# Hybrid decoder trunk on one core: the samples' value projection of the HGRN2 layer with high and low parts stacked in one stationary tile, and its halves joined on ACT and DVE

## What is computed

```python
def hgrn2_mixer(x, s0, lb, w_in, norm_g, w_out):
    q, f, v, gate = jnp.split(x @ w_in, 4, axis=-1)        # each 2048 wide, 16 heads of 128
    forget = lb + (1.0 - lb) * jax.nn.sigmoid(f)
    log_f = jnp.log(forget)
    k = (1.0 - lb) * jax.nn.sigmoid(-f)
    q = jax.nn.silu(q)
    o, s_new = gla_chunked(q, k, v, log_f, s0)              # chunks of 16 tokens, state (16, 128, 128)
    o = o * lax.rsqrt(jnp.mean(o * o, axis=-1, keepdims=True) + EPS)
    o = o.reshape(...) * norm_g * jax.nn.silu(gate)
    return o @ w_out, s_new
```

## Time and profile before

| what | value |
|---|---|
| time, median of 3 runs (lowest to highest) | 2019.58 (2018.29 to 2019.62) |
| span of the profiled execution, first to last instruction | 2015.7 |
| mean granted TensorE clock, as a share of full speed | 0.986 |
| PE busy / DVE busy / ACT busy / POOL busy | 97% / 62% / 46% / 50% of the span |
| HGRN2 stage, from the first projection to the last output product | about 1030 to 1468 of the span |

### The profile page before, as it was taken

The page is one execution under the profiler, slowest core; times in us unless marked ns, Lnnn a source line. Parts: engine busy times, 40 slices in busy tenths (PEclk is TensorE's granted clock), DMA queues, the critical chain, the costliest instruction groups (busy, mean ns, idle before and its releaser), DMA issues.

```text
span 2015.7 us, 35615 instructions
## 1 busy us (share of the span) xinstructions
PE 1951.5 (97%) x13890; PEld 1763.9 (88%) x13890; DVE 1244.4 (62%) x2220; ACT 930.6 (46%) x1557; POOL 1008.8 (50%) x1249
## 2 busy tenths in 40 slices
PE   7999999999999999999999999999999999999997
PEld 5998989798888988897889999999998889989976
DVE  5988342426887787755147777777454157874552
ACT  3676522334555555342354444443243347674333
POOL 4776704026555655250356666566631337776602
PEclk8999999999999999999999999999999999999998
DMA  4444476535444544487353444444586344445870
GB/s 130 149 147 135 135 250 231 208 105 174 124 116 132 151 132 140 138 297 241 113 170 108 130 130 130 137 136 146 165 313 211 132 148 141 135 148 166 292 231 27
DMA packets 332615, 324.64 MB, mean 161 GB/s; under 512 B 19768, under 2 KB 313056, under 8 KB 332448
## 3 DMA queue, kind: packets, MB, share of 16 engines
q1 hardware_dynamic: 330944, 321.49, 49.8%
q10 hardware_dynamic: 1504, 0.87, 0.2%
HBM read 292.16 MB, written 29.61 MB: 160 GB/s over the span
## 4 chain that ended last, share of the span: by engine, by line
PE 75%; DVE 14%; ACT 5%; issue 2%; DMA 2%; POOL 1%; SPq 1%; DVEq 0%; ACTq 0%
PE ps L773 10%; PE ps L774 10%; PE ps L778 10%; PE ps L1458 5%; PE ps L1467 4%; PE ps L1261 3%; PE ps L1524 2%; PE ps L888 2%; PE ps L763 2%; PE ps L765 2%; PE ps L764 2%; ACT wh L1713 2%; DVE work L2543 2%; PE ps L1602 1%; PE ps L1541 1%
## 5 line engine op out<-in xcount | busy, mean ns | idle before, releaser
L1693 POOL TENSOR_TENSOR wl<-raw,wh 128x256 fp32r<-128x256 f32 x1216 | 1003.3, 860 | 979.1 <-ACT wh L1713 978.9
L1713 ACT ACTIVATE wh<-raw 128x1024 fp32r<-128x1024 f32 x304 | 311.8, 1053 | 202.1 <-PE ps L778 49.8
L773 PE MATMUL ps<-Hh,wh 128*128 128x320 f32 x1200 | 372.2, 324 | 2.8 <-DVE work L2563 0.9
L774 PE MATMUL ps<-Hl,wh 128*128 128x320 f32 x1200 | 360.4, 314 | 0.0
L773 PEld LDWEIGHTS ps<-Hh,wh 128*128 128x128 f32 x1200 | 230.0, 192 | 11.3 <-DVE work L2427 2.3
L774 PEld LDWEIGHTS ps<-Hl,wh 128*128 128x128 f32 x1200 | 230.4, 192 | 2.1
L2258 DVE TENSOR_SCALAR work<-ps 128x512 f32<-128x512 f32 (+8 forms) x220 | 100.3, 474 | 170.9 <-PE ps L871 39.8
L778 PE MATMUL ps<-Hh,wl 128*128 128x320 f32 x1200 | 201.1, 310 | 0.0
L778 PEld LDWEIGHTS ps<-Hh,wl 128*128 128x128 f32 x1200 | 183.2, 189 | 0.1
L773 PE MATMUL ps<-Oh,wh 128*128 128x320 f32 x512 | 152.2, 310 | 3.7 <-DVE Ol L3004 3.7
L774 PE MATMUL ps<-Ol,wh 128*128 128x320 f32 x512 | 151.1, 308 | 0.0
(11 more groups left out here) (439 smaller groups left out, 3922.0 us busy)
## 6 DMA issues: line engine op xcount, KB each, us to landing
raw<-rg_w_in SPq DMA_DIRECT2D x128, 256.0 KB, 3.5
raw<-hg_w_in SPq DMA_DIRECT2D x128, 256.0 KB, 4.8
raw<-ssd_w_in SPq DMA_DIRECT2D x96, 256.0 KB, 3.9
work<-cache_mem_k SPq DMA_DIRECT2D x40, 512.0 KB, 6.3
work<-cache_mem_v SPq DMA_DIRECT2D x40, 512.0 KB, 5.1
raw<-rg_w_out SPq DMA_DIRECT2D x64, 256.0 KB, 3.6
raw<-x_w_k SPq DMA_DIRECT2D x64, 256.0 KB, 3.6
raw<-x_w_v SPq DMA_DIRECT2D x64, 256.0 KB, 3.7
```

The source lines that it names most:

```text
L773: pe.matmul(ps[:, bank, 0:n], high(half, k), mh[:, k, 0:n], start=(k == 0), stop=False)
L774: pe.matmul(ps[:, bank, 0:n], high(half, k), ml[:, k, 0:n], start=False, stop=False)
L1693: ins = pool.tensor_tensor(out, src, wh[:, parted(n) % HALVES, r:r + 2].bitcast(F32), ALU.subtract)
L1713: act.activation(wh[:, nx.n % HALVES], raw[:, slot, :, half * P:(half + 1) * P], ACT.Copy).then_inc(hi_ready, 1)
```

## The change

Before group 0 ACT and DVE build `hg_stack`, [128, 8, 128]: for each k the samples' 64 high columns beside their 64 low columns. `take_v(i, 2)` then uses it as the one stationary tile, with two products for each k (by the high and by the low weights). High rows come out on partitions 0 to 63 and low rows on 64 to 127 of the same bank, and their sum is v. ACT copies partitions 64 to 127 to `hg_v[0:64]`, and DVE adds partitions 0 to 63 of PSUM (`joined`). It is now this DVE instruction that raises `hg_v_read`. The rounding into `hg_vh` moves into ACT's next round (`round_v`), and the DMA between partitions is gone. To make room, `hg_K` is laid out without its unused quarter, as 14 rows of 64 columns, and its memsets are gone.

```diff
+            hg_stack = layout.enter_context(nc.sbuf_tensor("hg_stack", [P, KD, P], F32R))
...
-        hg_K = [c(9, P), c(9, P), c(9, P), c(9, P)]
+        hg_K = [c(14, 64), c(14, 64), c(14, 64), c(14, 64)]
+        hg_K_all, hg_K_late = [K[:, 0:9, :] for K in hg_K], [K[:, 9:14, :][:, ::-1] for K in hg_K]
...
# PE, take_v
+                    if T == 2 and i == 0:
+                        pe.wait_ge(*past("hg_stacked", 2))
                     for k in range(KD):
+                        if T == 2:
+                            pe.matmul(out, hg_stack[:, k, :], both(k), start=(k == 0), stop=False)
+                            mm = pe.matmul(out, hg_stack[:, k, :], rest_of(k), start=False, stop=(k == KD - 1))
+                            continue
...
# PE, turn_and_score
-                        pe.transpose(ps[:, 5, T * P:(T + 1) * P], hg_K[2 * h + T][:, 8, :], ident[:])
+                        pe.transpose(ps[:, 5, T * P:(T + 1) * P], hg_K[2 * h + T][:, 8:10, :].rearrange("p a c -> p (a c)"), ident[:])
...
-                                               hg_K[2 * h + T][:, c, 0:w], start=True, stop=True)
+                                               hg_K[2 * h + T][:, c:18 - c:17 - 2 * c, :] if w == P else hg_K[2 * h + T][:, c, :], start=True, stop=True)
...
# ACT
+                def round_v(i):
+                    act.wait_ge(*past("hg_v_read", i + 1))
+                    act.activation(hg_vh[0:64], hg_v[0:64, 2, :], ACT.Copy).then_inc(S("hg_v_high"), 1)
...
                     if i:
+                        round_v(i - 1)
                         scores_by_query(i - 1, 0)
...
-                    act.activation(hg_v[64:P, 2, :], ps[64:P, a + 1, 0:256], ACT.Copy).then_inc(S("hg_v_read"), 1)
-                    act.wait_ge(*past("hg_v_read", i + 1))
-                    steps.did(act.activation(hg_vh[64:P], hg_v[64:P, 2, :], ACT.Copy))
-                    steps.sync()
-                    act.dma_start(hg_v[0:64, 2, :], hg_v[64:P, 2, :]).then_inc(S("hg_v_twice"), 16)
+                    act.activation(hg_v[0:64, 2, :], ps[64:P, a + 1, 0:256], ACT.Copy).then_inc(S("hg_v_low"), 1)
...
+                act.wait_ge(*past("h_high", 5 * KD))
+                act.activation(hg_stack[:, :, 0:64], Hh[:, :, SEQ:NT].bitcast(F32), ACT.Copy).then_inc(S("hg_stacked"), 1)
                 for i in range(GROUPS):
                     body(i)
+                round_v(7)
...
# DVE
                 wait("h_ready", 5 * KD)
+                copy(hg_stack[:, :, 64:P], Hl[:, :, SEQ:NT].bitcast(F32)).then_inc(S("hg_stacked"), 1)
...
-                        wait("hg_v_twice", 16 * (i + 1))
-                        did(tt(hg_v[sm, 2, :], hg_v[sm, 2, :], hg_vh[sm].bitcast(F32), SUB))
+                        wait("hg_v_high", i + 1)
+                        did(tt(hg_v[sm, 2, :], hg_v[0:64, 2, :], hg_vh[0:64].bitcast(F32), SUB))
...
+                def joined(i):
+                    wait("hg_v_low", i + 1)
+                    tt(hg_v[0:64, 2, :], hg_v[0:64, 2, :], ps[0:64, 2 * (i % 2) + 1, 0:256], ADD).then_inc(S("hg_v_read"), 1)
+
                 for i in range(GROUPS + 1):
                     a = 2 * (i % 2)
+                    if i:
+                        joined(i - 1)
                     if i < GROUPS:
                         wait("hg_g_sig", i + 1)
...
-                    if i == 0:
-                        for K in hg_K:
-                            did(dve.memset(K[:, 0:4, 64:P], 0.0))
```

More of the change, by code:

```diff
@@ L153, in trunk @@
                            ("sn_full", "xs_full"), ("sn_read", "xs_read"), ("ssq_full", "xt_full"), ("v_read", "xt_read"),
-                           ("vm_ready", "xw_ready")):
+                           ("vm_ready", "xw_ready"), ("v_high", "y_done"), ("v_low", "z_sig"), ("stacked", "z_read"),
+                           ("raw_full", "raw_full"), ("raw_read", "raw_read")):
             shared["hg_" + hgrn] = ("sd_" + ssd_, 1, GROUPS)
@@ L368, in trunk @@
         hg_v = c(3, 256)
-        c(NB + 4, P)
+        c(NB + 4 + KD, P)
         hg_kt, hg_kx = c(2, P), par[:, 3, :]
         hg_D = c(4, 72)
-        hg_K = [c(9, P), c(9, P), c(9, P), c(9, P)]
+        hg_K = [c(14, 64), c(14, 64), c(14, 64), c(14, 64)]
+        hg_K_all, hg_K_late = [K[:, 0:9, :] for K in hg_K], [K[:, 9:14, :][:, ::-1] for K in hg_K]
         hg_att = [c(NT), c(NT)]
@@ L2835, in keys @@
                         k = hg_k[:, h, T * P:(T + 1) * P].rearrange("p (c s) -> p c s", s=16)
-                        K = hg_K[2 * h + T].rearrange("p a (c s) -> p a c s", s=16)
+                        early, late = (v[2 * h + T].rearrange("p a (c s) -> p a c s", s=16) for v in (hg_K_all, hg_K_late))
                         d = hg_D[:, 2 * h + T, :].rearrange("p (a b) -> p a b", b=8)
-                        did(tt(K[:, :, 0:4], k[:, 0:4].unsqueeze(1).broadcast_to([P, 9, 4, 16]), wide(d[:, :, 0:4], 16), MUL))
-                        return tt(K[:, 4:9, 4:8], k[:, 4:8].unsqueeze(1).broadcast_to([P, 5, 4, 16]), wide(d[:, 4:9, 4:8], 16), MUL)
+                        did(tt(early, k[:, 0:4].unsqueeze(1).broadcast_to([P, 9, 4, 16]), wide(d[:, :, 0:4], 16), MUL))
+                        return tt(late, k[:, 4:8].unsqueeze(1).broadcast_to([P, 5, 4, 16]), wide(d[:, 4:9, 4:8], 16), MUL)
                     did(keys(0, 0))
```

## The result

The changed kernel takes 2052.64 (median of 4, 2050.59 to 2053.04), the kernel before 2019.60 in the same session: ratio 1.0165, 95% interval 1.0142 to 1.0188. It is slower, by 33. The profiled execution took 2053.04 with a span of 2051.3, 35.6 longer than before.

The account below looks back on a forecast made before the run. PE's own work and DVE's loop (47.5 a round) were taken as nearly equal bounds, with the late join binding afterwards. 5.2 + 1.7 + 23.8 - 1.6 + 2.7 + 1.7 = 33.5 more gave 2053; range 2034 to 2062.

Parts of the forecast that it names:

- The place of the join: Top of DVE's next round: the add releases v at 1118.3, so PE idles 5.4 and starts q 4.5 later.
- The round: Groups 1 to 7: 48.9 at full clock plus 1.7 and 0.85 for slow clock, 51.45 against 47.48.
- the 0.85: PE from take_q to v: half of 1.7 for a second slow stretch, part of which coincides with the first loss.
- The sum: Whole kernel: 5.2 + 1.7 in round 1, 23.8 in six rounds, -1.6 + 2.7 + 1.7 at the end, 33.5 more.
- The saving of the products: PE's pass for v: eight products fewer a group, 0.96 each group, 7.7 in all if nothing else held.
- rival 1: Join ready in time, loop through stores and weights binds at 47.0: faster, 2015, or 2012 if all 7.7 arrive; chance 0.06.
- the 21.0: From the end of DVE's chain through stores, loads and splits until the next v may start: 21.0.
- The clock: PE behind each stall: idle time brings a slow clock, charged at 1.7 each, so a stall costs more than its length.
- rival 2: The stall at the join comes without a slow clock behind it: 14.8 more, 2034; chance 0.17.
- Keys and memsets at nothing: DVE's eight key products stay at 7.1 a round under the new layout, and the four removed memsets were hidden.
- The 11 of slack behind ACT's half: ACT's copy to other partitions: 0.38, at most doubled, with 11 between its end and DVE's arrival, so it costs nothing.
- stack and rounding at nothing: Stack copies run during group 0's gate and q; round_v (0.4) stands where ACT waits for PE's scores: both cost nothing.

Follow-up runs that it names:

- the early join: Changed kernel with the DVE add moved into keys_of, between its first four key products and the product of q with the decays: ratio 0.994 to the kernel before.
- two products only: Kernel before without the product of low samples by high weights for the samples' v, 64 products fewer: ratio 0.9943.
- the kernel with v first: Kernel before with the block of v weights issued on SP ahead of the store and load of the second head's states: ratio 0.9956.
- the two stretches of 304.8 and 304.4: Both with the v weights' block first on SP: changed kernel with add in keys_of, 0.991; kernel before without low samples by high weights, 0.9898.
- the filled kernel: Changed kernel with 36 unused products of 192 columns on PE ahead of its wait for hg_v_read in rounds 1 to 7: ratio 1.016 to the kernel before.
- the join one step earlier: Changed kernel with the DVE add placed ahead of new_state(j, 1, 1): ratio 1.0111 to the kernel before.

## Why the prediction was right, step by step

**The place of the join: right, and shown.** The wait alone makes 1.38% of the 1.65% in the old kernel, and moving the same instruction to an earlier place turns 1.65% more into 0.6% less.

**The round: right in kind, two terms off.** The forecast was 4.4 + 21.6 + 0.4 + 22.5 at full clock, and 1.7 + 0.85 for the clock, 51.45; the measured round is 51.20. Its terms from the rows above: v to `scored` 1207.24 - 1202.85 = 4.4; DVE's chain 1229.34 - 1207.24 = 22.1 (0.5 more than taken); the join and its signal 0.46; PE from q to v 24.25, where I had 25.05. The term that was wrong is the 0.85. The second slow stretch did come in every round, but in the half where PE waits for DVE anyway. For that reason PE idled 3.8 and not 5.4, and 2.6 and not 3.6 ahead of the third `take_out`. The chain, 0.5 longer than taken, made up for more than half of the 0.85.

**The sum.** Round 1: 6.9 forecast, 8.3 measured. `take_q(1, 0)` was 6.2 later, less the 0.7 by which the whole stage began later, and 5.2 was forecast for it. The missing 1.0 is DVE's: two products of round 0, q by the decays and the one behind it, took 1.37 and 0.81 where they had taken 0.82 and 0.28, here before and then after:

```profile
1066.65 0.82 DVE L2844 TENSOR_TENSOR work<-work 128x640 f32<-128x640 f32 x1
1067.38 0.28 DVE L2845 TENSOR_TENSOR later<-work,hg_en 128x128 f32<-128x128 f32 x1
```

```profile
1067.38 1.37 DVE L2858 TENSOR_TENSOR work<-work 128x640 f32<-128x640 f32 x1
1068.67 0.81 DVE L2859 TENSOR_TENSOR later<-work,hg_en 128x128 f32<-128x128 f32 x1
```

The other 8.3 - 6.2 = 2.1 came behind `take_q`, after 7.03 of idle time, with the clock at 0.50 for 5.0 (the two rows from 1075.50); I had taken 1.7. Six rounds: 23.8 and 22.3. End: 1.1 and 1.6, and 1.7 and 1.4 behind it. Not forecast: 0.7 ahead of the stage and 1.2 after it. That the total came within 0.5 (33.5 for 33.0 on the medians) is in part luck: these terms cancel.

**The saving of the products and rival 1: mis-sized.** The forecast itself does not use this loop, as the join binds first. I held that the loop through store, load and weights binds at 47.5, so that only 5 of the 7.7 would arrive. The runs showed 10.2 on the stretch and 11.5 in time. The step that failed is the 21.0 from DVE's chain to v. I read it off round 1 alone, where `out_hs_p` landed after 5.15. With the early join it lands after 3.24, and in two of the four rounds whose v waits for its weights the way is 19.0, so that the loop is 4.4 + 22.2 + 19.0 = 45.6 (in the other two it is 19.6 and 19.8, with a slower load of weights). With two products only, the rounds that waited so are 45.7 to 46.0 long. In the kernel before, the store took 5.1 to 5.2 in three of six rounds, the one of the earlier trace rows and these two, and 3.2 to 3.7 in the others:

```profile
1260.64 5.17 DMA out_hs_p<-work
...
1356.31 5.11 DMA out_hs_p<-work
```

Those three rounds are just the ones whose v waited for the weights (47.5, 47.6 and 47.0 long). In the other three PE had no idle time, and they were 46.6, 48.1 and 48.1 long, as the rounds of 45.0 of the kernel with v first are with one or two slow stretches. The rounds that I took for one loop's length were a mixture; the sum of 47.5 and the mean of 47.48 agreed by chance. Even the 45.6 of the early join is such a mixture: two of its rounds had no idle time ahead of v, and 44.0 with one slow stretch is 45.6 too. Why the store has two prices stays open: it never took more than 3.7 in the early and the two-product kernels, took 5.2 in one round of the changed kernel, and 5.1 in two rounds with the new layout and in three of the kernel before with v first. Nothing here tells what it collides with.

**The clock: right in kind.** That the stall drags the clock down was seen twice before the change and holds in every round after it. With the same products on PE, PE was busy 18.4 longer in the stretch by the slow clock, but not all of that lengthens the rounds. My estimate of what does is 6 x 1.55 by the filled kernel's rounds and 2.1 in round 1, some 11 of the 41.8 that the late join costs. The page "TensorE: Matmul & The Clock Gate" of the Trainium skill (section "What's actually happening") says that activity releases the throttle; the filled waits agree, and rival 2's 2034, which this rule spoke against, did not come. The row at 1290.50, at the half clock with PE busy all through, is not explained by that.

**Keys and memsets at nothing: right**, 0.9991. The 11 of slack behind ACT's half, and stack and rounding at nothing: right, by the two stretches of 304.8 and 304.4; ACT's copy to other partitions took the same 0.38.

## What to carry to other kernels

A signal that moves from one engine to another moves to that instruction's place in the new engine's order: read off the new engine's timeline when it gets there, and not when its operands are ready. Here an add of 0.41 placed behind 22 of other work cost a stretch of seven rounds 41.8, where the work that it enabled saved 10; the same add in the middle of that work cost nothing that shows. The clock makes a stall dearer than its length, in steps, so a change of such a wait can move a round by less than its size or by several times it (1.3 earlier gave 0.5 and 3.0 here, 0.73 later gave 0.7 and up to 3.5). And before a loop's length is taken from a chain of waits, look at more than one round: two different bounds can have the same mean.

## What was not expected of the hardware

- The clock falls without idle time too. In the row of the filled kernel at 1290.50 PE was busy all through at a mean clock of 0.52, behind 16 products of 8 columns and a few of 128. Which rounds have such a stretch differs between kernels: of the last two stretches shown, the first has two rounds of 45.6 and the second one, and all others are of 44.0 or 44.1.
- Idle time of 2.4 was followed by no slow stretch in three rounds of the join one step earlier, and 3.08 by none in round 1 of the filled kernel; 2.07 and 1.80 in the kernel before were followed by one each, and the 3.8 of the changed kernel by one in all six rounds. The length alone does not decide.
- A store of 128 KB lands after 3.2 to 3.7 or after 5.1 to 5.2, with one of 4.0 in between (join one step earlier), in otherwise equal rounds.
- `q` times the decays (128x640) takes 0.82 in each of six rounds before and 1.36 in each of six after; the layout and the instruction are the same. The chain's length changed by less than that. In both traces and all eight rounds this product and the one behind it took the high price just where one of POOL's subtractions was already running when they started, and the low one where none was or where the two started within 0.01 (POOL's then took 1.42 and not 0.79). The high price is a fixed amount more and not a ratio: 0.28 became 0.83, 0.48 became 1.02, 0.76 became 1.29 and 0.82 became 1.36, about 0.54 each time. No run isolates it, but it fits that the keys' layout was worth nothing.
